# Two weight tiles side by side at the start, casts ahead of the first root, one copy moved

## The reference

```python
def pool_layer(x, norm_g, w_in, w_group, scale, w_out):
    h = rmsnorm(x, norm_g)
    uz = h @ w_in
    u, z = uz[..., :POOL_WIDTH], uz[..., POOL_WIDTH:]
    ug = u.reshape(B, S, N_POOL_GROUPS, POOL_GROUP)
    pooled = jnp.stack([causal_window_mean(ug[:, :, g], w)
                        for g, w in enumerate(POOL_WINDOWS)], axis=2) - ug
    mixed = jnp.einsum('bsgc,gcd->bsgd', pooled, w_group).reshape(B, S, POOL_WIDTH) * scale
    y = mixed * jax.nn.silu(z)
    return x + y @ w_out
```

## Time and profile before

| | us |
|---|---|
| median of 3 runs | 1297.62 (1297.41 to 1298.44) |
| the profiled execution, first to last instruction | 1296.9 |
| between that span and the median | 0.7 |
| TensorE busy | 1287.1 |
| VectorE busy | 909.7 |
| ScalarE busy | 605.3 |
| POOL busy | 467.2 |

### The profile page before, as it was taken

The page is one execution under the profiler, slowest core; times in us unless marked ns, Lnnn a source line. Parts: engine busy times, 40 slices in busy tenths (PEclk is TensorE's granted clock), DMA queues, the critical chain, the costliest instruction groups (busy, mean ns, idle before and its releaser), DMA issues.

```text
span 1296.9 us, 18193 instructions
## 1 busy us (share of the span) xinstructions
PE 1287.1 (99%) x7006; PEld 1097.8 (85%) x7006; DVE 909.7 (70%) x1266; ACT 605.3 (47%) x999; POOL 467.2 (36%) x208
## 2 busy tenths in 40 slices
PE   9999999999999999999999999999999999999998
PEld 7887888898778888888889788898879999998886
DVE  7999826899292466656498674567989999985442
ACT  5223323435343466656654445578464444443223
POOL 2444544455444442452555343323430000015441
PEclk9999999999999999999999999999999999999999
DMA  4333423224723422326143345443323333323331
GB/s 164 98 98 106 121 91 98 72 91 116 290 81 98 135 59 83 82 62 216 49 146 114 115 149 146 133 113 114 98 65 131 98 99 119 110 84 112 114 97 66
DMA packets 47875, 143.66 MB, mean 111 GB/s; under 512 B 6032, under 2 KB 6032, under 8 KB 47024
## 3 DMA queue, kind: packets, MB, share of 16 engines
q1 hardware_dynamic: 43984, 129.88, 32.7%
q10 hardware_dynamic: 3808, 12.64, 2.7%
HBM read 121.46 MB, written 10.49 MB: 102 GB/s over the span
## 4 chain that ended last, share of the span: by engine, by line
PE 74%; issue 13%; POOL 7%; DVE 2%; ACT 1%; DMA 1%; SPq 0%; POOLq 0%; ACTq 0%
PE bank L2101 23%; PE bank L2103 23%; PE bank L2102 23%; POOL w_lo L701 7%; PE bank L2334 2%; PE bank L2323 1%; PE bank L2324 1%; DMA raw<-stream 1%; DMA x<-x_in 1%; PE bank L2125 0%; PE bank L2479 0%; PE bank L2480 0%; DVE zv L1834 0%; PE bank L2653 0%; ACT f_prob_t L993 0%
## 5 line engine op out<-in xcount | busy, mean ns | idle before, releaser
L701 POOL TENSOR_TENSOR w_lo<-raw,w_hi 128x1024 fp32r<-128x1024 f32 (+1 forms) x146 | 372.8, 2558 | 524.8 <-ACT w_hi L769 524.7
L769 ACT ACTIVATE w_hi<-raw 128x1024 fp32r<-128x1024 f32 x149 | 156.0, 1053 | 167.6 <-PE bank L2103 87.9
L746 POOL TENSOR_TENSOR w_lo<-raw,w_hi 128x1024 fp32r<-128x1024 f32 x22 | 53.6, 2441 | 263.0 <-DVE w_lo L1958 204.5
L2101 PE MATMUL bank<-pool_xg,w_hi 128*128 128x512 f32 x248 | 98.6, 398 | 0.2 <-POOL w_lo L701 0.2
L2102 PE MATMUL bank<-pool_xg,w_hi 128*128 128x512 f32 x248 | 98.1, 396 | 0.0
L2103 PE MATMUL bank<-pool_xg,w_lo 128*128 128x512 f32 x248 | 98.1, 396 | 0.0
L2101 PE MATMUL bank<-right,w_hi 128*128 128x256 f32 x336 | 94.4, 281 | 0.0
L2103 PE MATMUL bank<-right,w_lo 128*128 128x256 f32 x336 | 94.1, 280 | 0.0
L2102 PE MATMUL bank<-right,w_hi 128*128 128x256 f32 x336 | 94.1, 280 | 0.0
L2040 DVE TENSOR_TENSOR act<-acts,act 128x512 fp32r<-128x512 f32 x22 | 47.6, 2166 | 51.1 <-ACT act L1222 51.1
L2101 PE MATMUL bank<-y_hi,w_hi 128*128 128x512 f32 (+1 forms) x216 | 81.0, 375 | 0.0
(11 more groups left out here) (449 smaller groups left out, 3722.9 us busy)
## 6 DMA issues: line engine op xcount, KB each, us to landing
raw<-stream SPq DMA_DIRECT2D x187, 512.0 KB, 3.6
raw_x<-stream SPq DMA_DIRECT2D x18, 512.0 KB, 4.9
spill<-x ACTq DMA_DIRECT2D x2, 2048.0 KB, 7.8
xg_spill<-mla_xg ACTq DMA_DIRECT2D x2, 2048.0 KB, 12.0
rope_q<-turned_hl SPq DMA_DIRECT2D x64, 64.0 KB, 2.5
zx<-xg_spill SPq DMA_DIRECT2D x2, 1536.0 KB, 9.5
stacked<-fq SPq DMA_DIRECT2D x24, 128.0 KB
stacked<-fk SPq DMA_DIRECT2D x24, 128.0 KB
```

Of the source, the lines that this page charges most:

```text
L701: pool.tensor_tensor(w_lo[:, j % RING, 0:width], raw[:, j % RAW, 0:width], plain(w_hi[:, j % RING, 0:width]), ALU.subtract).then_inc(tile_ ...
L746: pool.tensor_tensor(w_lo[:, s, 0:D], raw[:, d % RAW, 0:D], plain(w_hi[:, s, 0:D]), ALU.subtract).then_inc(tile_lo, 1)
L769: act.activation(w_hi[:, t % RING, 0:width], raw[:, t % RAW, 0:width], ACT.Copy).then_inc(tile_hi, 1)
L2101: pe.matmul(target, a_hi, b_hi, start=start, stop=False)
```

## The change

- SP's first loads: the second weight tile is cut in two halves as the first is. The order is half of tile 0, x's first quarter, first half of tile 1, second quarter, second halves of tiles 0 and 1, third and fourth quarters. Before it was half of tile 0, first quarter, second half of tile 0, the other quarters, tile 1. The first half of tile 1 signals on `gain_in`, a semaphore that is used again at the end.
- ScalarE and VectorE cast and cut the first half of tile 1 ahead of chunk 2, and both second halves ahead of chunk 4.
- TensorE: `first_two_tiles` takes the place of `first_tile` and the projection of tile 1. It goes by pairs of chunks, tile 0 and then tile 1, each with all three products. FILL is 3. The same 48 matmuls are done.
- ScalarE: the cast of tile 2 stands behind the second square (before: the fourth), that of tile 3 behind the sixth (before: the last), that of tile 4 ahead of the root (before: behind it).
- TensorE: the mean stands ahead of chunk 6 of tile 2 (before: ahead of chunk 4).
- In the first output projection, the third copy stands ahead of step 11's cast (before: behind it).

```diff
-FILL = 6
+FILL = 3
...
-            for i in range(4):
-                sp.dma_start(x[:, 2 * i:2 * i + 2, :], x_in[:, 2 * i:2 * i + 2, :]).then_inc(x_loaded[i], 16)
-                if i == 0:
-                    sp.dma_start(raw[:, 0, HALF_D:D], stream[0, :, HALF_D:]).then_inc(tile_loaded[0], 16)
-            sp.dma_start(raw[:, 1, 0:D], stream[1]).then_inc(tile_loaded[1], 16)
...
+            sp.dma_start(*x_0).then_inc(x_loaded[0], 16)
+            sp.dma_start(raw[:, 1, 0:HALF_D], stream[1, :, 0:HALF_D]).then_inc(half_loaded_1, 16)
+            sp.dma_start(*x_1).then_inc(x_loaded[1], 16)
+            sp.dma_start(raw[:, 0, HALF_D:D], stream[0, :, HALF_D:]).then_inc(tile_loaded[0], 16)
+            sp.dma_start(raw[:, 1, HALF_D:D], stream[1, :, HALF_D:]).then_inc(tile_loaded[1], 16)
+            sp.dma_start(*x_2).then_inc(x_loaded[2], 16)
+            sp.dma_start(*x_3).then_inc(x_loaded[3], 16)
...
-            split_tile("pool_u", 0, -2)
             for k in range(DC):
                 if k >= 3:
                     act.wait_ge(n.summed, k - 2)
                 act.activation(pool_sq[:, k % 2, :] if k else pool_sqsum[:], x[:, k, :], ACT.Square).then_inc(n.squared, 1)
-                if k == 3:
+                if k == 1:
                     split_tile("pool_u", 0, -1)
+                if k == 5:
+                    split_tile("pool_u", 0, 0)
 
             for n in range(PC):
-                split_tile("pool_u", 0, n)
+                if n > 1:
+                    split_tile("pool_u", 0, n)
                 if n == 0:
+                    split_tile("pool_u", 0, 1)
                     norm_root(norm["pool"])
...
                 for k in range(first + 1, PC):
+                    if k == 11 and pooling:
+                        copy_first(copies.index(k))
                     split_tile(stage, 0, k)
-                    if k in copies:
+                    if k in copies[:2]:
                         copy_first(copies.index(k))
...
+            def first_two_tiles(n):
...
+                pe.wait_ge(half_lo, 1)
+                by_high(0, (0, 1))
+                by_low(0, (0, 1))
+                for i in range(FILL):
+                    pe.matmul(bank[7][:, 0:P], ones[:], ones[:], start=True, stop=True)
+                pe.wait_ge(half_lo, 2)
+                by_high(1, (0, 1))
+                by_low(1, (0, 1))
+                by_high(0, (2, 3))
+                by_low(0, (2, 3))
+                by_high(1, (2, 3))
+                by_low(1, (2, 3))
+                for chunks in ((4, 5), (6, 7)):
+                    for j in range(2):
+                        pe.wait_ge(tile_lo, j + 1)
+                        by_high(j, chunks)
+                        last = by_low(j, chunks)
...
-                if k == DC // 2:
+                if k == DC - 2:
                     mean(n.summed, DC - 1, pool_sqsum[:], bank[MEAN_BANK], n.mean)
```

More of the change, by code:

```diff
@@ L468, in build @@
         summed, combined = sem("weights_summed"), sem("products_combined")
-        copied, COPIED_BEFORE = half_hi, 1
-        last_gained, GAINED_BEFORE = half_lo, 1
+        copied, COPIED_BEFORE = half_hi, 2
+        last_gained, GAINED_BEFORE = half_lo, 2
         t_summed, T_SUMMED = pooled_ready, PC
@@ L579, in _ @@
             sp.dma_start(raw[:, 0, 0:HALF_D], stream[0, :, 0:HALF_D]).then_inc(half_loaded, 16)
-            for i in range(4):
-                sp.dma_start(x[:, 2 * i:2 * i + 2, :], x_in[:, 2 * i:2 * i + 2, :]).then_inc(x_loaded[i], 16)
-                if i == 0:
-                    sp.dma_start(raw[:, 0, HALF_D:D], stream[0, :, HALF_D:]).then_inc(tile_loaded[0], 16)
-            sp.dma_start(raw[:, 1, 0:D], stream[1]).then_inc(tile_loaded[1], 16)
+            quarters = (x[:, 2 * i:2 * i + 2, :] for i in range(4)), (x_in[:, 2 * i:2 * i + 2, :] for i in range(4))
+            x_0, x_1, x_2, x_3 = zip(*quarters)
+            sp.dma_start(*x_0).then_inc(x_loaded[0], 16)
[5 more added lines that the diff above has]
+            sp.dma_start(*x_3).then_inc(x_loaded[3], 16)
             def load(turn, j):
@@ L800, in _ @@
                 if k == 2:
-                    act.wait_ge(tile_loaded[0], 16)
-                    act.activation(w_hi[:, 0, HALF_D:D], raw[:, 0, HALF_D:D], ACT.Copy).then_inc(tile_hi, 1)
+                    act.wait_ge(half_loaded_1, 16)
+                    act.activation(w_hi[:, 1, 0:HALF_D], raw[:, 1, 0:HALF_D], ACT.Copy).then_inc(half_hi, 1)
+                if k == 4:
+                    for t in range(2):
+                        act.wait_ge(tile_loaded[t], 16)
+                        act.activation(w_hi[:, t, HALF_D:D], raw[:, t, HALF_D:D], ACT.Copy).then_inc(tile_hi, 1)
                 act.wait_ge(x_loaded[k // 2], 16)
                 act.activation(pool_xg_hi[:, k, :], x[:, k, :], ACT.Copy, scale=col("pool_norm", k)).then_inc(n.xg_hi, 1)
-            split_tile("pool_u", 0, -2)
             for k in range(DC):
@@ L1498, in _ @@
                 if k == 2:
-                    dve.wait_ge(tile_hi, 1)
-                    dve.tensor_tensor(w_lo[:, 0, HALF_D:D], raw[:, 0, HALF_D:D], plain(w_hi[:, 0, HALF_D:D]), ALU.subtract).then_inc(tile_lo, 1)
+                    dve.wait_ge(half_hi, 2)
+                    dve.tensor_tensor(w_lo[:, 1, 0:HALF_D], raw[:, 1, 0:HALF_D], plain(w_hi[:, 1, 0:HALF_D]), ALU.subtract).then_inc(half_lo, 1)
+                if k == 4:
+                    for t in range(2):
+                        dve.wait_ge(tile_hi, t + 1)
+                        dve.tensor_tensor(w_lo[:, t, HALF_D:D], raw[:, t, HALF_D:D], plain(w_hi[:, t, HALF_D:D]), ALU.subtract).then_inc(tile_lo, 1)
                 low_chunk(n, k, pool_xg_hi, pool_xg_lo, lambda c: col("pool_norm", c))
-            dve.wait_ge(tile_hi, 2)
-            dve.tensor_tensor(w_lo[:, 1, 0:D], raw[:, 1, 0:D], plain(w_hi[:, 1, 0:D]), ALU.subtract).then_inc(tile_lo, 1)
             for k in range(DC):
@@ L2071, in _ @@
                 act_low(d)
-            dve.wait_ge(gain_in, 16)
+            dve.wait_ge(gain_in, GAIN_BEFORE + 16)
             def final_block(b):
@@ L2210, in _, with by_high, by_low @@
                 pe.matmul(bank[7][:, 0:P], ones[:], ones[:], start=True, stop=True)
[L2212 to L2227, removed]
+            def first_two_tiles(n):
+                def by_high(j, chunks):
+                    for k in chunks:
+                        pe.wait_ge(n.xg_hi, k + 1)
+                        hi, lo = wblock(j, k)
+                        pe.matmul(bank[j][:], hi, pool_xg_hi[:, k, :], start=k == 0, stop=False)
+                        pe.matmul(bank[j][:], lo, pool_xg_hi[:, k, :], start=False, stop=False)
+                def by_low(j, chunks):
+                    for k in chunks:
+                        pe.wait_ge(n.xg_lo, k + 1)
+                        last = pe.matmul(bank[j][:], wblock(j, k)[0], pool_xg_lo[:, k, :], start=False, stop=k == DC - 1)
+                    return last
+                pe.wait_ge(half_lo, 1)
[15 more added lines that the diff above has]
+                        last = by_low(j, chunks)
+                        if chunks[-1] == DC - 1:
+                            last.then_inc(tile_used, 1)
```

7 lines of the change are left out of this document (4 added, 3 removed).

## The result

| | before | after |
|---|---|---|
| median, us (11 runs each, beside each other) | 1297.98 (1296.56 to 1299.69) | 1301.43 (1300.65 to 1302.33) |
| span of the profiled execution, us | 1296.9 | 1300.6 |
| TensorE busy, us | 1287.1 | 1288.3 |

The ratio is 1.0028 (95%: 1.0020 to 1.0036). The change costs 3.5 us; 1296.25 had been predicted, 1.4 us faster than before, and the range ended at 1297.8.

What follows compares the result with a forecast made beforehand. TensorE, busy 1287.1 of 1296.9 us, was taken as the bound. The copy's 1.43 less 0.06 at the start gave 1.37 us: span 1295.5, median 1296.25 with 0.7 between them; range 1295.2 to 1297.8.

Steps and rivals of the forecast that it cites:

- Tiles 0 and 1: TensorE's first two tiles, done side by side: tile 2 could start at 18.7, 1.5 us earlier.
- Rival (c): The loads at the start pay for being cut: the mean 2.2 us later, 1298.4 us in all; chance 0.05.
- The sum of squares: VectorE's adds for the mean: POOL holds two, so TensorE waits from 22.9 to 24.8, costing 1.9 us.
- the seventh add: Last add on pool_sqsum ahead of the mean: follows the sixth, held until 23.95, and ends at 24.7.
- the start: Everything up to tile 4: even at -0.06 us (+1.5, -1.9, +0.37), with ends of -0.6 to +0.2.
- Tile 4's wait: TensorE's wait at tile 4 for POOL's low part: it goes, a gain of 0.37 us.
- the copy: Third copy, first output projection, moved ahead of the cast: TensorE gains 1.43 us near 299, lower bound 1.2.
- Casts ahead of the root: ScalarE casts tile 4 at about 22, POOL cuts it by 25.9, so TensorE's 0.37 us wait goes.
- Pooling: VectorE's pooling behind a root 1.8 us late: first chunk takes 6.6 us instead of 8.7, nothing late behind it.
- Rival (b): The copy's gain is taken back by VectorE or by a wait the trace hides: 1297.6 us; chance 0.14.
- (a): The adds aren't held: mean on time at 22.9, 1.8 us from the start, 1.4 from the copy, 1294.4; chance 0.14.

Runs made afterwards that it cites:

- 2: The changed kernel with the cast of tile 4 back behind the root; 1299.7 us, ratio 1.0013 against the kernel before.
- 9: The changed kernel with only POOL held back, waiting for the last add of squares before its piece of tile 4; 1297.59 us, ratio 0.9997.
- experiment 3: The changed kernel with 17 more filler matmuls on ones ahead of the mean; 1299.79 us, ratio 1.0013.
- 8: The changed kernel with tile 3's cast behind the last square and tile 4's cast behind the root; 1297.52 us, ratio 0.9994.
- 4: The changed kernel with tile 3's cast behind the last square, tile 4's still ahead of the root; 1295.66 us, ratio 0.9980.
- experiment 6: The changed kernel with the mean moved on from tile 2's chunk 6 to tile 3's chunk 4; 1299.57 us, ratio 1.0009.
- experiment 5: The changed kernel with the third copy back behind the cast; 1302.18 us, ratio 1.0032.
- 10: The changed kernel with only POOL held back, waiting for the last add of squares before its piece of tile 3; 1295.73 us, ratio 0.9985.

## Why the prediction was wrong

**Tiles 0 and 1.** Right: tile 2 at 18.80 against 18.7, with the gains of x ending at 13.57 as forecast (13.5). Rival (c), that the loads pay for being cut, is refuted by the same row:

```profile
10.97 2.60 ACT L814 ACTIVATE pool_xg<-x,cols 128x512 fp32r<-128x512 f32 x4 [0.19 <-DMA x<-x_in]
```

**The sum of squares.** The mechanism was right and the chain was followed correctly for two holds: POOL at 15.55 and 21.0 in the forecast, 16.00 and 21.45 in the trace (0.45 later with the cast of tile 2, which its load let start at 14.79 and not at 14.4). The price of two holds was right as well: 1.9 us of waiting was forecast, and the two kernels with two holds show 2.2 and 2.3. **The step that failed is the seventh add.** The prediction set it at 24.0 to 24.7, free. A few paragraphs further, it had POOL cut tile 4 from 23.4 to 25.9. The add lies inside that piece, and by the prediction's own rule it had to be held until about 26.4. The piece had been booked as a gain at tile 4 (0.37) and never laid on VectorE's timeline. Experiments 2 and 9 show it: without that piece among the adds the wait is 2.3 and 2.2, with it 4.0.

**The clock.** The second failed step is one that wasn't there. No case of the prediction had a fall of TensorE's clock, since before has none to show at a wait of this length. It cost 2.8 us in after's profiled execution, more than the third hold (2.1), and experiment 3 shows it alone.

**The size of the miss.** The sum had -1.37; measured at the last tile is +3.77, so 5.14 us are to be found. The wait for the sum was 4.0 instead of 1.9 (2.1), the clock 2.8 (experiment 3), and the start gave 0.1 less. Tile 4's wait (0.47 for 0.37), the tiles up to the copy (+4.93 to +4.85) and the copy were each 0.1 better than forecast. That makes 4.7; the late drift of 0.4 (+3.34 to +3.77) makes 5.1. The drift is the least sure part: its piece near 950 us is a wait for ffn_xg that stands in after and in experiment 2 and not in 3, and why wasn't settled.

**Casts ahead of the root.** The forecast of tile 4's wait was right in kind: it goes (+5.40 to +4.93). But the cast is worth more than before's 0.37 shows. With the new order and the cast behind the root, tile 4 waits 1.6 us, whether the mean is on time (8) or 2.3 late (2). At tile 4 itself the cast ahead is worth 1.8 us (4 against 8) and 1.9 (9 against 2).

**Pooling.** "Nothing is late behind it" was right. VectorE's first and second chunk of it end on these rows, where the earlier trace rows has 28.86 and 37.58:

```profile
34.13 0.69 DVE L1541 TENSOR_TENSOR u_pad<-bank,inv 128x512 f32<-128x512 f32 x1 [0.56 <-DVE u_pad L1528]
...
40.76 0.69 DVE L1541 TENSOR_TENSOR u_pad<-bank,inv 128x512 f32<-128x512 f32 x1
```

The chunk takes 6.6 us, as forecast, and 8.7 before. It starts 5.3 us later than before and ends 3.2 later, while TensorE's tiles are 4.9 later, so no tile waits. With the root late and the tiles early, as in experiment 6, the reserve is used up.

**The copy.** Right: 1.43 forecast, 1.5 in after and 1.5 alone, kept to the end. Rival (b) is refuted. In after the cast behind the copy found its load landed and ran right behind it, so the copy delayed it by some 0.3 us, without effect. The only reserve is experiment 5, where the unmoved copy cost 0.4 less.

**The rivals and the range.** (a) had the mean on time, 1.8 us from the start and 1.4 from the copy. As a forecast of this kernel it fell. Experiments 4 and 10, with one held add, have the mean on time by other means, and show 1.4 or 1.3 and 1.5. The slower side was looked for in the loads (0.05), where nothing was. It lay in the forecast's own mechanism with one hold more. The lower and upper ends for the start, -0.6 to +0.2, came from loads a little early or late; they did not ask what one more held add would do. At full clock that alone is 2.1 us, 1298.3, already outside the range; only with the half clock besides does the sum come to some 1301, near what was measured.

## What to carry to other kernels

When an operation of POOL is moved, lay each of its pieces on VectorE's timeline and mark every add with two operands in SBUF that starts inside one: here each such add ended behind the piece, and with pieces back to back, one behind each. A cast that is moved forward for the sake of its consumer also moves the POOL work that follows it, and here the work to protect was a reduction on which a matmul waits. A wait of TensorE that grows past those seen in the profile of before should be priced with a second case, at half clock; if such a wait can't be removed, matmuls that do nothing are worth their place in it.

## What the runs showed of the hardware

- VectorE's add with two operands in SBUF took 2.46 and 2.64 us beside POOL's subtraction and 0.69 without it. Of the 84 adds on pool_sqsum in the twelve traces, 22 meet a piece of POOL: they took 2.45 to 2.85 us, and each ended 0.55 us behind that piece. The other 62 took 0.68 to 0.70. Experiments 9 and 10 make this causal: only POOL's start was moved.
- Once a wait of 4.0 us had lowered TensorE's clock (half from 25.7 to 32.5, the wait being 23.2 to 27.2), it stayed low while TensorE was busy again, for 5.3 us and 11 matmuls. With a wait of 3.6 us the half clock came only once TensorE had gone on working (27.0), and lasted 3.4 us. So the clock's loss was 2.7 to 2.8 us in one execution and 1.7 in another with the same instructions up to 270 us.
- Waits of 2.2 and 2.3 us (experiments 9 and 2) left the clock at 1.00 in the traces.
- By the mean clock of each execution (0.998 or less) it fell in 10 of 11 executions of after, 5 of 5 of experiment 5, 4 of 11 of experiment 2, 2 of 10 of experiment 9, and in none of the 75 of the other experiments. It also did in 4 of the 82 executions of the kernel before that ran beside the experiments; they are its slowest (1300.4 to 1301.2). What decides it in a single execution isn't shown.
- The first two weight tiles and x in loads of half size and in another order cost nothing that can be seen: the last gain ended at 13.57 in after and from 13.24 to 14.02 in the ten traces with this order, where 13.5 was worked out from loads in a row at 1.38 us for 512 KB.
- Left open: the wait for ffn_xg near 950 us, which came and went between kernels that differ only in the first 30 us.
